# A product-key expert stage that begins with the first query block, with its v sums held in PSUM banks and its gathered rows in two rings

## The reference, cut to what matters

```python
def peer(h, w_q, sub_keys, expert_u, expert_v):      # 2 blocks of 128 tokens, 8 heads, top 16
    q = einsum("td,de->te", hb, w_q).reshape(tb, 8, 2, 128)
    scores = einsum("thpc,hpnc->thpn", q, keys32)     # 2 x 128 scores per head
    s_top, i_top = top_k(scores, 16)
    ...                                               # best 16 of the 16 x 16 sums: idx, gate
    u = take(expert_u, idx, axis=0)                   # rows of 1024 floats
    act = gelu(einsum("tkd,td->tk", u, hb))
    vv = take(expert_v, idx, axis=0)
    return einsum("tk,tkd->td", gate * act, vv)
...
x = x + peer(h2, ...)
return rms_norm(x, final_norm_g)
```

## Time and profile before

| | us |
|---|---|
| median of 3 runs | 3033.11 (3029.89 to 3041.18) |
| the profiled execution's own time | 3031.36 |
| its span in the profile | 3029.8 |

### The profile page before, as it was taken

How to read it: one execution, slowest core, us unless ns; L and a number is a source line. 1 busy time by engine, 2 the same in 40 slices (tenths; PEclk the granted TensorE clock), 3 DMA queues, 4 the chain that set the end, 5 groups by cost and what they waited for, 6 DMA issues and landing times.

```text
span 3029.8 us, 35271 instructions
## 1 busy us (share of the span) xinstructions
PE 2611.2 (86%) x14626; PEld 2157.7 (71%) x14626; DVE 1567.0 (52%) x3097; ACT 821.0 (27%) x1364; POOL 591.0 (20%) x540
## 2 busy tenths in 40 slices
PE   7999999999989999999989999979955565646566
PEld 7998888989989988889889978858832222222222
DVE  5442974535555545765345452451065656566654
ACT  4431024414443421043234313420121111111111
POOL 0000000000000000000000000000066776767665
PEclk9999999999999999999999999989977787878787
DMA  5576973034535569951135534414288998989896
GB/s 198 183 173 108 154 144 102 1 115 153 189 122 191 182 110 147 153 131 44 58 114 192 181 119 131 141 40 133 76 305 319 333 370 293 337 324 363 324 366 236
DMA packets 324722, 557.20 MB, mean 184 GB/s; under 512 B 16201, under 2 KB 245587, under 8 KB 324563
## 3 DMA queue, kind: packets, MB, share of 16 engines
q1 hardware_dynamic: 250834, 286.48, 35.5%
q0 software_dynamic: 73728, 268.47, 23.8%
HBM read 553.85 MB, written 1.05 MB: 183 GB/s over the span
## 4 chain that ended last, share of the span: by engine, by line
PE 74%; DVE 15%; issue 3%; another core or an unknown queue 2%; POOL 2%; ACT 2%; DMA 1%; SPq 0%; DVEq 0%; POOLq 0%
PE bank L323 30%; PE bank L349 8%; PE bank L350 8%; PE bank L351 8%; PE bank L2142 8%; PE bank L1002 3%; DVE expert_u_rows L2095 3%; POOL expert_u_rows L2082 1%; DVE gdn_conv L2031 1%; DVE gdn_conv L2028 1%; ACT residual L2127 1%; PE bank L597 1%; PE bank L823 1%; DVE gdn_conv L2055 1%
## 5 line engine op out<-in xcount | busy, mean ns | idle before, releaser
L2142 PE MATMUL bank<-proj,residual 128*128 128x512 f32 x1024 | 483.4, 636 | 330.4 <-ACT residual L2127 278.6
L323 PE MATMUL bank<-operand,weights 128*128 128x256 f32 x3456 | 754.8, 380 | 1.1 <-DVE operand L574 1.1
L323 PEld LDWEIGHTS bank<-operand,weights 128*128 128x128 f32 x3456 | 657.7, 191 | 93.5 <-issue 3.3
L2142 PEld LDWEIGHTS bank<-proj,residual 128*128 128x128 f32 x1024 | 208.1, 205 | 605.1 <-issue 314.9
L349 PE MATMUL bank<-operand_hi,weights_high 128*128 128x256 f32 x1408 | 399.2, 284 | 22.5 <-DVE cnv_dw_cols L525 15.7
L350 PE MATMUL bank<-operand_lo,weights_high 128*128 128x256 f32 x1408 | 398.0, 283 | 0.0
L351 PE MATMUL bank<-operand_hi,weights_low 128*128 128x256 f32 x1408 | 396.2, 281 | 0.0
L343 DVE TENSOR_TENSOR weights_low<-weights,weights_high 128x1024 fp32r<-128x1024 f32 x264 | 308.1, 1221 | 131.8 <-ACT weights_high L335 131.8
L631 POOL TENSOR_TENSOR residual<-residual,branch 128x512 f32<-128x512 f32 x12 | 15.3, 1272 | 1737.3 <-DVE branch L574 1737.3
L2082 POOL DMA_INDIRECT expert_u_rows<-in_peer_u,gdn_conv x256 | 297.2, 1161 | 162.3 <-issue 74.5
L2095 DVE CUSTOM_DVE_ANT_0 expert_u_rows<-expert_u_rows,branch 128x1024 f32<-128x1024 f32 x256 | 302.7, 1223 | 46.1 <-DMA expert_u_rows<-in_peer_u,gdn_conv 44.3
(11 more groups left out here) (351 smaller groups left out, 2934.9 us busy)
## 6 DMA issues: line engine op xcount, KB each, us to landing
weights<-in_ffn_w_in SPq DMA_DIRECT2D x88, 1024.0 KB, 5.0
weights<-in_mix_w_in SPq DMA_DIRECT2D x64, 1024.0 KB, 11.7
weights<-in_ffn_w_out SPq DMA_DIRECT2D x44, 1024.0 KB, 4.9
weights<-in_w_in SPq DMA_DIRECT2D x24, 1024.0 KB, 5.3
weights<-in_cnv_w_o SPq DMA_DIRECT2D x8, 1024.0 KB, 5.1
weights<-in_gdn_w_o SPq DMA_DIRECT2D x8, 1024.0 KB, 5.0
weights<-in_mix_w_out SPq DMA_DIRECT2D x8, 1024.0 KB, 5.2
weights<-in_peer_w_q SPq DMA_DIRECT2D x8, 1024.0 KB, 5.2
```

The source lines that it names most:

```text
L323: ins = t.matmul(out, raw[:, k, q * P:(q + 1) * P], x[:, k, :], start=(k == 0), stop=(k == KT - 1))
L2142: ins = t.matmul(m.bank[2 * p + half][:, :], K.diag[p][:, s, :], K.v[p][:, s, half * 512:half * 512 + 512], start=(s == 0), stop=(s == GRO ...
```

## The change

- The ring order becomes sub-keys, then `peer_q`. The keys are transposed on PE ahead of the norm (`tensor_sub_keys`), into `m.y`.
- The scores of a head are made between the query blocks: after block 0 those of head 0, after block h (h from 2) those of head h - 1, after the loop those of head 7. h is transposed after blocks 0 and 1, x after all scores. The query goes to `m.silu` and `m.gated` in turn; `m.proj` is free for rows.
- POOL starts as soon as turn 0 is chosen. u has 12 homes (8 in `m.proj`, 4 in the homes of weight blocks), v has 15 (8 and 7). Row r waits until row r - 12 was used in a dot (u) or row r - 15 was summed (v). The homes in the weight ring wait for query blocks 2, 2, 3, 3 (u) and 4, 4, 5, 5, 6, 6, 7 (v).
- PE adds all v rows of one half of the tokens up in the same two banks (0 and 1, then 2 and 3): 128 rows. DVE adds the banks to `x_tok` twice in all, at i = 18 and at the end. The final norm of the first half moves to i = 18.
- ACT does the exp of turn 0 at h = 2 and the gelu of group 0 at h = 5 of the query loop, and the diagonals of group 0 after that loop and the copies of x. It loads the square root's table between the gelu and the diagonals of group 31.

The core of the diff (the loops over homes and the moved loads are told above):

```diff
-                        ("w_out", 4), ("peer_q", 8), ("sub_keys", 1)):
+                        ("w_out", 4), ("sub_keys", 1), ("peer_q", 8)):
...
+        self.u = [(rows[:, s, :], None) for s in range(G)] + late[0:4]
+        self.v = [(rows[:, G + s, :], None) for s in range(G)] + late[4:11]
...
 def tensor_scores(X, m, S, K):
+    for h, _ in enumerate(tensor_blocks(X, m, S, ("peer_q", 2), HEADS, m.operand, S.out_act, normed_at(S, "norm2"))):
+        if h < 2:
+            for n in (2 * h, 2 * h + 1):
+                tensor_turn_quarter(X, m, S, "h", m.operand, n)
+        if h != 1:
+            tensor_head_scores(X, m, S, K, max(h - 1, 0))
+    tensor_head_scores(X, m, S, K, HEADS - 1)
+    for n in range(4):
+        tensor_turn_quarter(X, m, S, "x", m.x, n)
...
+def pool_rows(X, m, S, K, i, homes, landed, freed, table):
+    n, p = divmod(i, 2)
     X.pool.wait_ge(*S.choose.at(n, "chosen"))
     for s in range(GROUP):
+        r = i * GROUP + s
+        home, block = homes[r % len(homes)]
+        if r >= len(homes):
+            X.pool.wait_ge(*freed.at(*row_of(r - len(homes))))
+        elif block is not None:
+            X.pool.wait_ge(*S.used.at(block))
+        at = bass.IndirectOffsetOnAxis(ap=K.index[n % 2][:, p * GROUP + s:p * GROUP + s + 1], axis=0)
+        landed[r % len(homes)].by(X.gpsimd.indirect_dma_start(out=home, out_offset=None, in_=table, in_offset=at), r)
...
 def vector_group(X, m, S, K, i):
...
-    if i:
-        vector_add_group(X, m, S, K, i - 1)
...
 def tensor_group(X, m, S, K, i):
     w.wait_ge(*S.diag.at(i))
-    if i >= 2:
-        w.wait_ge(*S.taken.at(i - 2))
...
-                           start=(s == 0), stop=(s == GROUP - 1))
+                           start=(i % HALF == 0 and s == 0), stop=(i % HALF == HALF - 1 and s == GROUP - 1))
...
 def pool_experts(X, m, S, K, io):
-    X.pool.wait_ge(*S.score_pe.at("scores", 1, 3))
     for i in range(GROUPS):
-        pool_group(X, m, S, K, io, i)
+        pool_rows(X, m, S, K, i, K.u, S.u_in, S.dotted, io["peer_u_2"][0])
+        pool_rows(X, m, S, K, i, K.v, S.v_in, S.summed_v, io["peer_v_2"][0])
+HALF_DONE = HALF + 2
...
 def vector_experts(X, m, S, K):
...
+        if i == HALF_DONE:
+            vector_add_experts(X, m, S, K, 0)
+            vector_last_norm(X, m, S, K, 0)
+    vector_add_experts(X, m, S, K, 1)
 def scalar_experts(X, m, S, K):
     for i in range(GROUPS):
-        scalar_group(X, m, S, K, i)
+        if i:
+            scalar_gelu(X, m, S, K, i)
+        if i == GROUPS - 1:
+            scalar_sqrt_table(X, m, 11)
+        scalar_diagonals(X, m, S, K, i)
```

More of the change, by code:

```diff
@@ new lines, in tensor_sub_keys, with scalar_sub_keys @@
+def tensor_sub_keys(X, m, S):
+    b = RING.first["sub_keys", 2]
+    X.pe.wait_ge(*S.loaded[b % SLOTS].at(b))
+    for i in range(4):
+        X.bank_free(4 + i)
+        for j in range(4):
+            ins = X.tensor.transpose(m.bank[4 + i][:, j * P:(j + 1) * P], keys_slot(m)[:, 4 * i + j, :], m.ident[:, :])
+        S.used.by(ins, b) if i == 3 else S.score_pe.by(ins, "keys", i)
+        X.free[4 + i] = [S.score_act.at("keys", i)]
+def scalar_sub_keys(X, m, S, K):
+    for i in range(4):
+        X.act.wait_ge(*(S.used.at(RING.first["sub_keys", 2]) if i == 3 else S.score_pe.at("keys", i)))
+        S.score_act.by(X.scalar.copy(K.keys[:, 4 * i:4 * i + 4, :], m.four(4 + i)), "keys", i)
@@ new lines, in tensor_turn_quarter, with scalar_turn_quarter @@
+def tensor_turn_quarter(X, m, S, name, src, n):
+    half, q = QUARTERS[n]
+    X.bank_free(4 + n)
+    for k in range(4):
+        ins = X.tensor.transpose(m.bank[4 + n][:, k * P:(k + 1) * P], src[:, 4 * q + k, half * P:(half + 1) * P], m.ident[:, :])
+    S.score_pe.by(ins, name, n)
+    X.free[4 + n] = [S.score_act.at(name, n)]
+def scalar_turn_quarter(X, m, S, name, rows, n):
+    half, q = QUARTERS[n]
+    X.act.wait_ge(*S.score_pe.at(name, n))
+    S.score_act.by(X.scalar.copy(rows[:, half, q * 512:q * 512 + 512], m.bank[4 + n][:, :]), name, n)
@@ new lines, in tensor_head_scores @@
+def tensor_head_scores(X, m, S, K, h):
+    b = 3 if h % 2 == 0 else 4
+    X.bank_free(b)
+    X.pe.wait_ge(*S.out_act.at(RING.first["peer_q", 2] + h))
+    X.pe.wait_ge(*S.score_act.at("keys", 3))
+    for half in range(2):
+        for s in range(2):
+            ins = X.tensor.matmul(m.four(b)[:, 2 * half + s, :], K.q[h % 2][:, s, half * P:(half + 1) * P], K.keys[:, 2 * h + s, :],
+                                  start=True, stop=True)
+    S.score_pe.by(ins, "scores", h)
+    X.free[b] = [S.score_act.at("scores", h)]
@@ L1980, in scalar_scores @@
 def scalar_scores(X, m, S, K):
-    a, w = X.scalar, X.act
     first = RING.first["peer_q", 2]
-    for i in range(8):
-        scalar_take_block(X, m, S, first + i, m.proj[:, 2 * i:2 * i + 2, :])
-    for i in range(4):
-        w.wait_ge(*S.score_pe.at("keys", i))
-        S.score_act.by(a.copy(K.keys[:, 4 * i:4 * i + 4, :], m.four(i)), "keys", i)
-    for half in range(2):
-        for i in range(4):
-            w.wait_ge(*S.score_pe.at("scores", half, i))
-            S.score_act.by(a.copy(K.scores[:, 16 * half + 4 * i:16 * half + 4 * i + 4, :], m.four(4 * half + i)), "scores", half, i)
@@ L1992, in scalar_scores @@
-    for name, rows in (("h", K.h_tok), ("x", K.x_tok)):
-        for n, (half, q) in enumerate(QUARTERS):
-            w.wait_ge(*S.score_pe.at(name, n))
-            S.score_act.by(a.copy(rows[:, half, q * 512:q * 512 + 512], m.bank[4 + n][:, :]), name, n)
+    for h in range(HEADS):
+        if h >= 2:
+            X.act.wait_ge(*S.score_pe.at("scores", h - 2))
+        scalar_take_block(X, m, S, first + h, K.q[h % 2][:, :, :])
+        if h < 2:
+            for n in (2 * h, 2 * h + 1):
+                scalar_turn_quarter(X, m, S, "h", K.h_tok, n)
+        if h != 1:
+            scalar_head_scores(X, m, S, K, max(h - 1, 0))
+        if h == 2:
+            scalar_choose(X, m, S, K, 0)
+        if h == 5:
+            scalar_gelu(X, m, S, K, 0)
@@ L2006, in vector_counting @@
     X.dve.wait_ge(*S.score_dve.at("counting"))
-    X.dve.wait_ge(*S.score_act.at("scores", 0, 0))
 class Steps:
@@ L2111, in vector_add_group @@
     for half in range(2):
         at = slice(half * 512, half * 512 + 512)
-        ins = X.vector.tensor_tensor(x[:, at], x[:, at], m.bank[2 * p + half][:, :], ALU.add)
-    S.taken.by(ins, i)
-def scalar_group(X, m, S, K, i):
-    a, w, p = X.scalar, X.act, i % 2
-    w.wait_ge(*S.dotted.at(i, GROUP - 1))
-    if i >= 2:
-        w.wait_ge(*S.weighed.at(i - 2))
-    S.gelu.by(a.activation(K.acts[p], K.dots[p], ACT.Gelu), i)
-    w.wait_ge(*S.weighed.at(i))
+        ins = X.vector.tensor_tensor(x[:, at], x[:, at], m.bank[2 * t + half][:, :], ALU.add)
```

165 lines of the change are left out of this document (76 added, 89 removed).

## The result

| | before, us | after, us |
|---|---|---|
| median (4 runs each) | 3033.22 (3029.89 to 3041.18) | 2962.65 (2953.7 to 2966.59) |
| profiled execution | 3031.36 | 2963.78 |
| span | 3029.8 | 2962.2 |

A forecast was written before the change was run, and what follows sets the result against it. DVE's order was taken to make the loop, POOL's issue close behind. Head start -42.8, fifteen pairs -61.8, norm +3, end -1.4 sum to -103.0 us: profiled execution 2928.4, median 2930 us, range 2885 to 2985.

The forecast's parts named there:

- Steps 1 and 2: Start: key transposes ahead of the norm shift everything by 1.9 us; first gather issued at about 2161.3 instead of 2208.18.
- Step 3: Start up to u row 16 (group 2): that row issued at 2211.5 instead of 2254.3, a gain of 42.8 us.
- Just in time, and next to be late: Start: choice 1, begun after ACT's gelu at about 2188, is done by 2210.
- Step 4: Expert loop, fifteen pairs: POOL's issue becomes the loop at 45.9 us per pair, 688.5 against 750.3, so -61.8 us.
- port term: Expert loop: POOL's issues lengthened beside dots, 4.2 us per pair for back-to-back dots plus 2.0 for paced ones.
- POOL hardly waits: Expert loop: dots and v sums are there when POOL needs them, the first sum by 10 for need at 20.
- Step 5: Norm at i = 18: about 6 us on DVE once, of which 0 to 6 comes through; taken as +3 us.
- Steps 6 and 7: End: table load +1.2, only one half left -2.6, together -1.4 us; PE sums kept in banks: nothing.
- The third one: Rival, expert loop: stays near its length, choices of 21 us fill DVE; 48.1 or 50 per pair, 2963 to 2991 us; chance 0.20.
- The second: Rival, expert loop: DMA is the loop at a lower rate, 47 us per pair, 2946 us; chance 0.06.
- The rival that dots do not slow the issue: Expert loop: DMA or POOL's bare rate is the loop, 40.8 us per pair, 2854 us; chance 0.12.
- The slower rival: Expert loop: with 15 v homes, last v rows wait for the sum of the group just before; 3040 us; chance 0.03.

## Why the prediction was right or wrong

**Steps 1 and 2, keys and first choice: right.** The keys cost 1.91, the choice 10.24, and the first gather stood at 2160 to 2161 in the runs that had no shift (2160.39 and 2161.27 among them). The 5.7 us of the profiled run lie ahead of the change, and the kernel before has 5.3 of the same kind in its second profile.

**Step 3, the head start: right in kind, too large.** It gave 25.0 of 42.8 us at u row 16. The shift is 5.7 of the difference and 12.1 remain. Some 7 of them go with the stops from 2193 to 2208. The rest is step 3's own: even on the second chip the two runs with 15 homes for v and the tokens in PSUM had u row 16 at 2215.89 and 2217.04, 4 to 6 us past the forecast, because row 15 waited for the first sum, and with 16 homes it went out at 2205.78, ahead of the forecast. "Just in time, and next to be late" was said of choice 1; v row 15 was the one to say it of.

**Step 4, fifteen pairs: this is the step that failed.** On a chip with stalls removing the adds did what the step said: in the run with the bank sums alone the wait for dots fell to 14 us, and nearly the whole gain of the loop is there, with eight homes for u. That the four extra homes carry the loop is not borne out; whether they are worth some us is open. The sum was off in two terms of opposite sign. The port term was put at 6.2 per pair and measured 3.9. The price of an issue beside dots was right, 1.98 us; how many issues pay it was not. DVE waited 128 us for rows, so that fewer dots ran beside issues; that this is the reason is argued and not shown, since with half rows, where DVE waits for rows more often still, the term is 6.3.

And "POOL hardly waits" was put at 0 and measured 3.7 per pair. The step had the sum that a v row needs "there by 10", ten us ahead of the need. But twelve times in the profile, for 39.8 us in all, POOL stood in front of a v row while PE worked through its matmuls with pauses of 1 to 4 us, and twice, for 17.5 us, in front of a choice of 31 us. The prediction read the wait for dots in the earlier trace rows as the work of DVE's order, and saw in the stretched choices of the earlier trace rows only a reason for DVE to be late. They were the mark of a second thing, which holds DVE, PE and ACT now and then. In the kernel before it reached POOL through the dots, in the changed one through PE's sums. 3.7 less 2.3 is 1.4 per pair or 21 us over fifteen; the norm gave back its 3, and the loop was 17.5 us longer than forecast. That the forecast came out so near owes something to luck: two misses of 35 and 55 us lay against each other. By the estimate for the second chip the step's cause is wrong too as a general one: where nothing stalls, the adds cost the loop next to nothing.

**Step 5, the norm: nothing instead of 3 us.** The adds and the norm of the first half held DVE from 2650.35 to 2655.64, 5.3 us, and POOL had no gap of over 0.6 us between 2647 and 2717.

**Steps 6 and 7, end and banks: right**, -1.3 for -1.4; DVE waited for PE at an add once, at the end.

**The rivals.** The third one, by which the loop stays near its length because choices stretch, came closest (2963 for its shorter end), but by another way. Choices of 31 us did occur, yet only 17.5 us of POOL's time went into waiting for them; the rest were waits for PE's sums. The second has 47 us a pair for a slower DMA, and 47.3 were measured, but by luck: the DMA's share was 0.95 at 358 GB/s, 44.5 us a pair if it were full, and with half the bytes the pair was still 46.1. The rival that dots do not slow the issue is wrong: 1.98 and 1.99 stand in the profile after as before, and the run with the tokens in PSUM shows what it would have given, 40.5 per pair on the second chip and 45.8 on the third. The slower rival had the waits for PE's sums in the loop, and that is where most of POOL's lost time lay; but it put them down to the fifteenth home, and with sixteen they were longer (89.4 us on the third chip). The home itself is paid for once.

**What stays open** is what the stalls are. Shown: PE, DVE and ACT pause for 1 to 6 us under no named cause, PE between matmuls of one row, and POOL then waits in front of v rows. The pauses are there on two chips, and in the first two profiles, and absent on a third chip that ran the same program. They were seen only while gathers run: the first choice takes 10.2 us in every profile, and before 2149 us no engine waits for "remote" in any. Choices are stretched less with half the bytes (195 us, where the two runs of the changed kernel's loop on that chip have 252 and 257) and most with the fullest stream (310). That they go with the chip and not with the full stream (C and not D) rests on one chip of three, and whether the chip or something that ran on it at the time is not known: what other cores did is not on record. Packets of the instruction queues were too few to be matched with them (6 or 7 and 12 or 13 in 550 us, on a stalling chip and on the other alike). No way to take them away within a kernel was tried.

## What to carry to other kernels

Before a wait is put down to the order of the instructions, look for pauses inside the records of the engine that is waited for: the same 41 steps in 10.4 us and in 31, or one matmul at a time. Such pauses do not go with the wait that showed them; here they moved from the dots to PE's sums. Where a gap has no named releaser, see which instructions it stands in front of, and what those wait for. An indirect gather issued by GpSimd beside VectorE work is cheapest where VectorE reads at most one operand from SBUF; here moving 1 MB of tokens to PSUM that PE had written there anyway took 21 us off the kernel with sixteen homes on one chip and, together with the sixteenth home, 31 off the changed kernel on another. A ring one home short of two groups cost its wait where the pipeline fills, 10 us, and not in each turn.

## What the runs showed of the hardware that was not expected

- The same program took 2929 us on one chip and 3029 and 3032 us on two others. The 100 us lie where the gathers run, as far as the profiles show: of the kernel with 16 homes and the tokens in PSUM, spans of 2856.9 and 2928.7 stand side by side, and from u row 16 to the last issue it differs by 76 us, ahead of that by 11, and at the end by -15.
- An indirect gather of 128 rows is issued in 0.94 us with 0.30 between two, alone or beside dots with one operand in PSUM, and in 1.99 beside dots with two in SBUF, at an unchanged 1.22 us per dot.
- Gathers of 4 KB rows hold 409 GB/s for 550 us. The Trainium skill (SBUF — State Buffer, A bandwidth-pool intuition that's wrong) gives about 358 GB/s for HBM to a core; the trace does not agree, with 409.
- Half the bytes per gather, with the same number of gathers, leaves the issue loop nearly where it was: 40.2 for 40.5 us a pair with the tokens in PSUM, 46.1 for 47.0 to 47.5 with both operands of the dots in SBUF.
- On two chips of three PE's matmuls, DVE's short steps and ACT's copies paused for 1 to 6 us at a time while gathers ran (16 stretches of 41 DVE steps: 243 to 310 us in the changed kernel and its variants with whole rows, 166 on the quiet chip). In the same profiles, from u row 16 on, no gap of POOL of over 0.6 us in front of a u row is called "remote".
